# First layer of a decoder trunk: normalize and turn six heads beside the last attention items, and move the last gate section into the norm's gap

## The reference, cut to what matters

```python
mod = silu(c) @ ada_w[i] + ada_b[i]                     # 6 sections of 1024 in a layer
sh_a, sc_a, g_a, sh_f, sc_f, g_f = split(mod, 6)
h = rmsnorm(x, norm_mix[i]) * (1.0 + sc_a) + sh_a
y = diff_attention(h, ...)                              # layer 0
    # 8 heads, 2 blocks of 128 queries each: p = softmax(q k / 8 - slope * dist)
    # o = (p[first] - lam * p[second]) @ v
    # o = rmsnorm(o, subln_g) * (1 - lam_init)          # over the 128 values of one head
    # return o.reshape(B, S, 1024) @ w_out
x = x + g_a * y
h = rmsnorm(x, norm_ffn[i]) * (1.0 + sc_f) + sh_f
x = x + g_f * moe(h, ...)
```

## Time and the profile before

| | |
|---|---|
| time, median of 3 runs | 1453.29 us (1452.13 to 1454.12) |
| time of the profiled execution | 1451.76 us |
| its span | 1450.0 us |
| PE busy | 1328.0 us (92% of the span) |
| DVE, ACT, POOL busy | 550.8, 444.5, 206.1 us |
| read from memory | 514.10 MB |
| mean granted clock of PE | 0.974 of full speed |

### The profile page before, as it was taken

The page is one execution under the profiler, slowest core; times in us unless marked ns, Lnnn a source line. Parts: engine busy times, 40 slices in busy tenths (PEclk is TensorE's granted clock), DMA queues, the critical chain, the costliest instruction groups (busy, mean ns, idle before and its releaser), DMA issues.

```text
span 1450.0 us, 32945 instructions
## 1 busy us (share of the span) xinstructions
PE 1328.0 (92%) x12029; PEld 875.3 (60%) x12030; DVE 550.8 (38%) x1217; ACT 444.5 (31%) x874; POOL 206.1 (14%) x657
## 2 busy tenths in 40 slices
PE   4899678999999999998789999789999999999996
PEld 2788366555455554554489989665555555555553
DVE  2565457233232332222443445473233223322333
ACT  3443333222122222221334454332222222222222
POOL 8000021111111111111000000011111111111110
PEclk9899988999999999999889999999999999999999
DMA  9999992999999999999985534529999999999994
GB/s 345 372 381 399 409 352 81 423 419 423 422 421 422 422 421 422 423 421 421 383 281 181 169 117 146 189 107 422 420 422 421 422 421 422 421 422 422 422 421 204
DMA packets 113082, 516.06 MB, mean 356 GB/s; under 512 B 9368, under 2 KB 46368, under 8 KB 63104
## 3 DMA queue, kind: packets, MB, share of 16 engines
q1 hardware_dynamic: 109920, 509.64, 87.6%
q0 software_dynamic: 2400, 3.49, 0.8%
q10 hardware_dynamic: 704, 2.10, 0.4%
HBM read 514.10 MB, written 1.09 MB: 355 GB/s over the span
## 4 chain that ended last, share of the span: by engine, by line
PE 72%; SPq 8%; DVE 5%; ACT 5%; DMA 5%; issue 3%; POOL 1%; ACTq 1%; DVEq 0%; POOLq 0%
PE bank L882 20%; PE bank L1059 15%; PE bank L1062 7%; PE bank L1080 7%; PE bank L994 6%; PE bank L1035 5%; SPq L336 5%; DMA ring<-in_exp_w_dram 4%; PE bank L1086 3%; PE bank L858 2%; SPq L339 2%; DVE arena L1487 1%; ACT arena L674 1%; DMA ring<-in_da_w_out_dram 1%; PE bank L1069 1%
## 5 line engine op out<-in xcount | busy, mean ns | idle before, releaser
L1059 PE MATMUL bank<-ring,arena 128*64 128x512 f32 x768 | 178.5, 605 | 13.1 <-DMA ring<-in_exp_w_dram 13.1
L1035 PEld LDWEIGHTS bank<-arena 128*128 128x128 bf16 x3264 | 142.1, 98 | 55.5 <-issue 55.0
L994 PE MATMUL bank<-arena_r 128*128 128x512 f32 x560 | 161.1, 418 | 3.0 <-DVE arena_r L1499 3.0
L1499 DVE TENSOR_TENSOR arena_r<-bank,arena_r 128x512 fp32r<-128x512 f32 x136 | 94.1, 692 | 154.1 <-ACT arena_r L686 154.1
L1035 PE MATMUL bank<-arena 128*128 128x64 bf16 (+1 forms) x3264 | 151.8, 207 | 0.0
L679 ACT ACTIVATE arena<-bank 128x256 f32<-128x256 f32 (+1 forms) x68 | 22.6, 333 | 386.9 <-PE bank L1059 269.8
L686 ACT CAST arena_r<-bank 128x512 fp32r<-128x512 f32 x136 | 79.7, 586 | 189.5 <-PE bank L1080 124.8
L994 PEld LDWEIGHTS bank<-arena_r 128*128 128x128 f32 x560 | 94.6, 188 | 60.0 <-issue 47.5
L882 PE MATMUL bank<-HH_r,ring_r 128*128 128x256 f32 x448 | 127.7, 285 | 0.0
L531 POOL TENSOR_TENSOR arena<-arena,pass_base 128x2 f32 x136 | 23.6, 197 | 732.2 <-PE bank L1046 727.1
L1059 PEld LDWEIGHTS bank<-ring,arena 128*64 128x64 f32 x768 | 56.5, 139 | 114.5 <-issue 113.9
(11 more groups left out here) (271 smaller groups left out, 2151.2 us busy)
## 6 DMA issues: line engine op xcount, KB each, us to landing
ring<-in_exp_w_dram SPq DMA_DIRECT2D x264, 1024.0 KB, 24.0
ring<-in_ada_w_dram SPq DMA_DIRECT2D x48, 1024.0 KB, 12.3
HH<-in_exp_w_dram SPq DMA_DIRECT2D x40, 1024.0 KB, 20.4
mods<-in_exp_w_dram SPq DMA_DIRECT2D x40, 1024.0 KB, 24.3
arena<-in_exp_w_dram SPq DMA_DIRECT2D x40, 1024.0 KB, 25.0
ring<-in_ret_w_in_dram SPq DMA_DIRECT2D x24, 1024.0 KB, 11.2
ring<-in_da_w_in_dram SPq DMA_DIRECT2D x12, 1024.0 KB, 16.4
ring<-in_ret_w_out_dram SPq DMA_DIRECT2D x8, 1024.0 KB, 4.9
```

The costliest lines, as they stand in the source:

```text
L994: ins = nc.tensor.matmul(banks[4 + NH * tc + hf][:, :], S[:, P * tc:P * tc + P], y[:, r, 512 * hf:512 * hf + 512], start=False, stop=(last ...
L1035: ins = nc.tensor.matmul(banks[2 - 2 * half][:, P * kk:P * kk + 2 * W], parts[:, tc, r, P * (4 * half + kk):P * (4 * half + kk + 1)], Pg[: ...
L1059: ins = nc.tensor.matmul(banks[1][W * i:W * i + W, :], xg[:, k, W * i:W * i + W], w13[j][:, k, :, :], start=(k == 0), stop=(k == KD - 1))
L1499: nc.vector.tensor_tensor(y[:, 1, 512 * hf:512 * hf + 512], banks[hf][:, :], y[:, 0, 512 * hf:512 * hf + 512], ALU.subtract).then_inc(u[f" ...
```

## The change

Four edits to layer 0, all in the hand-written order.

- **Order of the stream.** `LATER` becomes (0,2), (0,3), (0,4), then the six sections of layer 1, then (0,5), and the four tiles of (0,5) stand behind those of `w_out`. The section itself is computed in `moe` ahead of `turn_h`, once the first half of x is new. Its bias row gets a place of its own (`row5`), DVE adds it behind `low_part("shared", 0, 1)`, and POOL stores and spreads it later.
- **Six heads early.** The mean squares, roots, reciprocals and scaling of heads 0 to 5 (items 0 to 11) are done on ACT and DVE while items 14 and 15 are still under way; PE turns them (`turn_o(0)` to `turn_o(2)`) around `turn_a(15)`. Scaling is now two operations for six heads and two for the last two heads.
- **The projection begins with them.** ACT evicts and rounds the three banks, DVE takes the low parts, and `mix_out` of tile 0 is issued before the last two heads are turned; `turn_o(3)` follows tile 0.
- **Buffers.** The high parts of `w_out` lie in `HH` and `mods` instead of the arena, and bank 0 takes the last two heads.

```diff
-LATER = [(1, s) for s in range(6)] + [(0, 3), (0, 4), (0, 2), (0, 5)]
+LATER = [(0, 2), (0, 3), (0, 4)] + [(1, s) for s in range(6)] + [(0, 5)]
...
-    order += sum(later[6:], [])
-    order += [("mix_out", 0, i) for i in range(4)]
+    order += sum(later[6:9], [])
+    order += [("mix_out", 0, i) for i in range(4)] + later[9]
...
-                ("mix_out", 0): (arena_r[:, 4096:6144], arena_r[:, 10240:12288]),
+                ("mix_out", 0): (HH_r[:, 0:2 * D], mods_r[:, 3 * D:5 * D]),
...
+            ada_bank[9] = banks[4]
+            oT_bank = [banks[i] for i in (1, 2, 3, 0)]
...
-            nc.gpsimd.memset(nrowA, 0.0).then_inc(rows_zero, 1)
+            nc.gpsimd.memset(mods[:, 5 * D:5 * D + 768], 0.0).then_inc(rows_zero, 1)
...
-                               ada_b[0:1].rearrange("a (s q n) -> q a s n", s=6, q=4)[q, :, 2:6]).then_inc(rowsA_in, 16)
+                               ada_b[0:1].rearrange("a (s q n) -> q a s n", s=6, q=4)[q, :, 2:5]).then_inc(rowsA_in, 16)
+                pool.dma_start(row5[32 * q:32 * q + 1, 0, :], ada_b[0:1, 5 * D + 256 * q:5 * D + 256 * (q + 1)]).then_inc(rowsA_in, 16)
...
-            store_rows(1, 0, 6, 6)
-            store_rows(0, 2, 4, 10)
+            store_rows(0, 2, 3, 3)
+            store_rows(1, 0, 6, 9)
             pool.wait_ge(rows_stored, 128)
...
-            pool.wait_ge(o_sumsq, DA_ITEMS)
-            spread(0, 5, gates_in)
...
+            store_rows(0, 5, 1, 10)
+            pool.wait_ge(rows_stored, 192)
+            spread(0, 5, gates_in)
...
+                if l == 0:
+                    release_ada(9)
...
+            load_root_table()
+            act.wait_ge(o_meansq, 1)
+            nc.scalar.activation(early(rs), early(ss), ACT.Sqrt).then_inc(o_root, 1)
             square_o(12)
             release_ada(7)
             evict_aT(14)
             square_o(13)
+            round_w("mix_out", 0, 0)
+            evict_aT(15)
             release_ada(8)
-            evict_aT(15)
-            release_ada(9)
-            load_root_table()
...
+            square_o(14)
             round_w("mix_out", 0, 1)
-            for m in range(4):
+            for m in range(3):
+                evict_oT(m)
+            square_o(15)
+            for m in range(3):
+                round_oT(m)
+            act.wait_ge(o_meansq, 2)
+            nc.scalar.activation(last_heads(rs), last_heads(ss), ACT.Sqrt).then_inc(o_root, 1)
+            mixer_out(0, 0)
+            evict_oT(3)
+            round_oT(3)
+            for i in range(1, 4):
                 mixer_out(0, i)
...
+                if l == 0:
+                    pe.wait_ge(x_new, 1)
+                    ada(*LATER[9], ada_bank[9][:, 0:256])
                 turn_h()
...
-            turn_a(15)
-            later(9)
-            attend(15)
-            pe.wait_ge(o_normed, 1)
-            pe.wait_ge(bank_rows_read, len(LATER))
+            pe.wait_ge(s_ready, DA_ITEMS)
+            pe.wait_ge(o_normed, 1)
+            turn_o(0)
+            turn_a(15)
+            turn_o(1)
+            turn_o(2)
+            attend(15)
+            pe.wait_ge(o_ready, DA_ITEMS)
+            pe.wait_ge(bank_rows_read, 9)
             for i in range(4):
                 mix_out(0, i, 4, da_oT_of)
+                if i == 0:
+                    pe.wait_ge(o_normed, 2)
+                    turn_o(3)
...
+                if l == 0:
+                    later_rows(9)
...
+            mean_squares(early, DA_ITEMS - 4)
             later_rows(6)
             finish_a(14)
             keep_o(13)
             later_rows(7)
             finish_a(15)
+            dve.wait_ge(o_ready, DA_ITEMS - 4)
+            normalize_o(early, slice(0, DA_HEADS - 2), 1)
             keep_o(14)
             later_rows(8)
+            low_part("mix_out", 0, 0)
             keep_o(15)
+            mean_squares(last_heads, DA_ITEMS)
+            for m in range(3):
+                low_oT(m)
             dve.wait_ge(o_ready, DA_ITEMS)
+            normalize_o(last_heads, slice(DA_HEADS - 2, DA_HEADS), 2)
+            low_part("mix_out", 0, 1)
+            low_oT(3)
             low_part("mix_out", 0, 2)
             low_part("mix_out", 0, 3)
```

More of the change, by code:

```diff
@@ L306, in trunk @@
                 turns.append(("ada", 2 * (i // 3) - 2 + i % 3))
-        turns += [("ada", k) for k in range(6, len(LATER))]
+        turns += [("ada", k) for k in range(6, 9)]
         proj0_bank = {i: banks[7 * (n % 2)] for n, (kind, i) in enumerate(turns) if kind == "proj"}
@@ L457, in store_rows @@
                 pool.wait_ge(rows_ready, ready)
-                rows = browA[:, first - 2:first - 2 + count, :] if l == 0 else browB[:, first:first + count, :]
+                rows = browB[:, first:first + count, :] if l == 1 else row5 if first == 5 else browA[:, first - 2:first - 2 + count, :]
                 for q in range(4):
@@ L1522, in later_rows @@
                 if k == 0:
+                    dve.wait_ge(rowsA_in, 16 * 12)
+                if k == 3:
                     dve.wait_ge(rowsB_in, 16 * 12)
[L1524 to L1526 removed]
+                row = browB[:, sec, :] if l == 1 else row5[:, 0, :] if sec == 5 else browA[:, sec - 2, :]
                 dve.wait_ge(ada_done, 2 + k + 1)
```

70 lines of the change are left out of this document (34 added, 36 removed).

## The result

The changed kernel took 1444.22 us (median of 6 runs, 1439.25 to 1448.15) against 1452.79 us of the kernel before (6 runs, 1452.13 to 1454.12). The ratio is 0.9938, 95% interval 0.9918 to 0.9957. Run twice more without any edit, on other chips, it gave 1440.23 and 1443.52, at ratios of 0.9911 and 0.9920. So it is faster by 9 to 13 us, each time with an interval clear of 1. The forecast was 1440.5, within 1437 to 1445.

The account below looks back on a forecast made before the run. It took the weight stream and the serial chain behind `w_out` to bound the kernel ahead of the loop. Terms -12.75 + 0.45 + 0.3 - 1.0 + 0.25 = -12.75 us gave 1440.5 us against the median, range 1437 to 1445.

Parts of the forecast that it names:

- The start of the projection: Output projection of layer 0: starts at 173.6 us, -12.75 us, with the first tile of `w_out` landing at 165.45.
- the tiles follow each other evenly: Rival on the stream into `w_out`: its first tile lands at 164.0, total 1439.0 us; chance 0.15.
- POOL's larger memset: Kernel's opening: last memset grows from 256 to 768 columns, +0.25 us (0 to 0.3); four more small loads hidden.
- The wait before tile 2: Inside the output projection: PE newly waits for tile 2's rounding and low part, +0.3 us, bounds 0 and 1.
- The slow stretch: Projection's first microseconds at clock 0.53 stay as they are; gone entirely saves about 1.9 us, longer costs 0.5.
- `turn_h` at full clock: Transposes after the norm: PE kept busy by the gate section, so they run at full clock, -1.0 us (-1.0 to 0).
- The added row: One addition on DVE of about 0.4 us in the routing's chain: costs 0, up to 0.4 if PE gets ahead.
- PE gets ahead: Rival: logits at full clock gain 0.4 us through the routing, with no slow stretch in the projection; 1438.3 us, chance 0.08.
- The loop keeps its length: Loop over the experts: same length, only starting sooner, so each microsecond saved ahead of it shortens the kernel by one.
- transfers hidden: Rival: `w_out` lands no sooner, only the overlap is gained, -2.5 us; 1450.8 us, chance 0.03.
- the gate section holds everything up: Rival ahead of `turn_h`: late section tiles delay norm, routing and loop; 1457 us or more, chance 0.03 with other waits.
- The gap hurts: Rival in the norm's gap: the section runs at half clock, 7.3 us for 3.66; 1442.8 or 1443.5 us, chance 0.12.

Follow-up runs that it names:

- stream_only: Changed kernel with all eight heads normalized and turned at once behind item 15, as before the change; 1445.10 us, ratio 0.9939.
- heads_only: Changed kernel with the tiles and section (0,5) put back ahead of `w_out`, leaving only the six early heads; 1453.17 us, ratio 1.0000.
- changed_again: Changed kernel without any edit, run beside two repaired kernels on one chip; 1443.52 us, ratio 0.9920.
- pool_start: Changed kernel with POOL's opening block as in the kernel before, the gate row's place zeroed and loaded later; 1443.05 us, ratio 0.9938.
- before_again: Kernel before the change, unedited, run again for a second profiled execution; 1452.44 us, ratio 0.9994.
- later_and_start: Changed kernel with POOL's memset of `y` waiting for `shT` and POOL's opening block as before the change; 1441.30 us, ratio 0.9908.
- after: First profiled execution of the changed kernel, against the kernel before; 1444.57 us, span 1442.8.
- memset_later: Changed kernel with one added line: POOL's memset of `y` waits until DVE has written `shT`; 1442.83 us, ratio 0.9925.
- memset_section: memset_later with the whole gate section waiting for the second half of x instead of the first; 1443.41 us, ratio 0.9926.
- spread_section: later_and_start with the gate section's 64 matmuls in four pieces of 16 over the norm's gap; 1439.85 us, ratio 0.9895.
- before: First profiled execution of the kernel before the change, unedited; 1451.76 us, span 1450.0.
- again: Changed kernel without any edit, once more for a second trace; 1440.23 us, ratio 0.9911, profiled execution 1447.92.
- held: Changed kernel with DVE waiting, ahead of the ranking's two compares, until POOL's iotas are done; 1450.99 us.

## Why the prediction was right, and where its steps failed

**The start of the projection: right, by two errors that cancel, and so by luck.** 173.49 for 173.6, and the first cast at 165.63 for 165.45. ACT's chain is as it was worked out, link by link: second cast 168.19 (168.03), evictions until 171.8 (171.7), 1.49 us from the first rounding to the first matmul. But 165.45 came from leaving the 4.04 us between the two matrices in place. They did not stay. The landings above are 2.5 us apart at that turn in the changed kernel, and in all other kernels with the tiles moved but one (`stream_only`, 3.8). In `heads_only`, with the order of before, the first tile of `w_out` lands 2.4 us behind the last of (0,5), and a step of 3.35 us lies inside (0,5). So the extra 1.5 us belong to no turn between matrices; what they belong to stays open. In the chance of 0.15 for *the tiles follow each other evenly* the mechanism was right. Its time was not: the tile in that place of the stream landed at 163.95 before and at 165.60 after, the stream being 1.65 us behind by then, which the prediction had at nothing. Some of it may go with the later first projection: `changed_again` and `pool_start`, which have that at 40.78 and 40.83, were 0.5 and 1.0 us behind. The rule of the Trainium skill, "DMA: Bandwidth & Descriptors", section "Queues, rings and completion order", by which the prediction had 2.56 us, agrees with the 2.54 us here; the 4.07 of before it does not give.

**POOL's larger memset: term mis-sized, 0.25.** The memset itself grew by 0.43 us (0.45 to 0.88; 0.3 estimated), and the first transposes came 0.35 later, DVE's low parts 0.25. The step that failed is "four more small loads from POOL are hidden". They push POOL's four selects of `decay` from 34.88 to 37.14, beside DVE's low parts of the first weights:

```profile
37.14 4.55 POOL L500 TENSOR_SCALAR_AFFINE_SELECT decay<-decay 128x256 f32<-128x256 f32 x4
```

```profile
35.83 3.21 DVE L1386 TENSOR_TENSOR mods_r<-mods,HH_r 128x512 fp32r<-128x512 f32 x4 [0.57 <-ACT HH_r L618]
38.96 2.48 DVE L1391 TENSOR_TENSOR ring_r<-ring,mods_r 128x2048 fp32r<-128x2048 f32 x1
```

Before, the selects took 2.44 us, the low parts 2.90 and 2.28. Each slows the other, and the first matmul comes 0.25 + 0.31 + 0.20 = 0.76 us later. Over all profiled executions it comes between 40.78 and 42.21 in nine with the larger block (mean 41.41) and between 40.55 and 40.83 in five with the old one (mean 40.74). So the term is 0.7 us on the mean for 0.25, but uneven: `changed_again` has 40.78 with the larger block. With the old block put back (`pool_start`) the selects took 1.91 and the low parts 2.87 and 2.28 again.

**Projection: 24.79 us for 24.4.** The wait before tile 2 is 0.32 (0.3 forecast), the four transposes cost 0.35 (0.45). Of the 1.14 us by which the projection grew, 0.47 are left: tiles 1 and 2 took 5.73 and 5.62 us for 5.44 each, and why stays open. The slow stretch was left as it was, and it was: the 24 matmuls of tile 0 took 7.34 us, the clock back by 177. `before_again` needs 24.72 us without any transposes between, as its clock rose later.

**`turn_h` at full clock: -1.0 not gained in the profiled execution.** It ran in 3.62 us at half clock. The step "PE is now busy until the equivalent of 213.7, so `turn_h` should still find the full clock" holds in some executions only. The 2.33 us of idle time that the prediction itself left behind the section are enough, in six of nine profiled executions, for `turn_h` to run slow. Where the clock holds, it is worth 0.86 us (6.66 from `turn_h` to the logits in `later_and_start`, 7.52 in after), so the size was about right and the certainty wrong.

**The added row, "0, and up to 0.4 if PE gets ahead": the wrong price.** Where PE does not get ahead, the 0.42 us cost nothing: DVE still waits 0.60 us for ACT before `shT` in after (0.81 before). Where PE gets ahead, the 0.42 us are not the price; the collision with POOL's memset is, and that is 3.84 us. The rival *PE gets ahead* (1438.3) therefore had an end that it did not name: a faster PE can make a slower kernel. Two of 17 executions of the changed kernel took 1448; of 19 with the memset behind `shT` (`memset_later`, `memset_section`, `later_and_start`, `spread_section`) none took over 1445.3. None of 19 against two of 17 could also be chance, and that the other long one had the same cause is not shown, as only one was profiled.

**From the logits to the loop, 0.46 us: put at nothing.** PE's first matmuls there ran at half clock until 4.5 us behind their start before, and until 6.1 us in after; PE was through with the up-projections 18.66 us behind the logits' start for 18.21. That is the 0.46.

**"The loop keeps its length": failed, by 1.9 us.** All three executions of the changed kernel need 481.9 to 482.1 from the loop's start to the next projection, both of the kernel before 480.24 and 480.28. In the loop the gathers of 128 columns (L1061) begin some 21 to 31 us apart, 17 times. The first 13 begin within 0.2 us of before's. Then single ones differ, in either direction: the 14th is 1.6 to 1.8 us later in the changed kernel, the 15th 1.3 to 1.4 sooner, the 17th within 0.25 again, and the next projection 1.7 to 1.9 later, while the bytes moved since the loop's start are the same to 0.1 MB at every 40 us. Such steps come between executions of one kernel too: the 16th is at 400.28 in after and at 401.99 in `again`. The moved tiles alone do not explain the end: `spread_section` has them and needs 480.34. What decides these steps stays open.

**Layer 1, 1.9 us, was not in the prediction at all.** Both losses are the clock again. By the one-microsecond stretches, it rises 3.0 and 3.2 us after layer 1's projection begins in the two executions of the kernel before, and 5.5 to 5.7 us after in the three of the changed kernel; at layer 1's logits it rises after 3.4 us in both of before, and after 4.9 to 5.0 in the changed kernel. Over all 14 profiled executions the length goes with the rise: 93.6 to 93.8 us to the retention with a rise after 3.0 to 3.6 us (`before`, `before_again`, `held`, `later_and_start`), 94.6 to 94.7 with one after 5.4 to 5.7 (the ten others). That is shown; what sets the rise is not. `heads_only`, with nothing moved in the stream, has the late one, and `later_and_start`, with everything moved, the early one, so it can be put down to no part of the change that was tried. One to three executions of each kernel are too few to say that it goes with the kernel.

The terms with what was measured: start of the projection -12.86 (forecast -12.75, with +0.25 for POOL apart, which the -12.86 contains), the projection itself +1.14 (+0.75), `turn_h` 0 (-1.0), from the logits to the loop +0.46 (0), behind it +4.06 (0): -7.2 in this pair of executions. Of the 4.5 us in the last two, 2.4 are matmuls at half clock and 1.9 the loop's end. The range reached up to 1445 for other reasons (a gap at half clock, the added row, the wait for tile 2); that the median lies inside it is in part luck. The medians differ by 8.6, 13.3 and 10.9 us on three chips, where the forecast had 12.8: one above, two below. The rivals *transfers hidden* and *the gate section holds everything up* are refuted: `w_out` lands 10.1 us sooner, and PE never waits for the section's tiles. These landed only at 190.3, though, not at 184: between 179.59 and 184.21 another queue, with the small transfers that POOL issues, took 42% of the transfer engines' time, and the tiles came 3.7 to 6.1 us apart. The margin was 8 us, not 14. (That rival's 1457 should read some 1456 by its own terms.) *The gap hurts* did not occur in the change itself (3.66 us, full clock), but was made to occur by a later start (5.35 us).

## What to carry to other kernels

An engine that gets ahead can meet another one that it never met before: for every instruction that becomes free sooner, look at what runs on DVE at that time when POOL is the one released, and tie a long memset to a point behind the short chain that others wait for. Count PE among the engines that can get ahead: its clock may rise 3 or 6 us into the same stretch of matmuls. A short stall on a chain that PE waits for costs more than its own length, since the matmuls behind it may run at half clock; filler work put at one end of the idle time did not keep the clock in most executions here, and four pieces laid over it did in the one that was profiled. Landing times of single transfers settle questions that the waits of an engine hide. And when a gain of 1% is followed through a long kernel, run both kernels a second time with a profile: here half of what was given back late was the moment at which PE's clock rose, which no edit that was tried accounts for.

## What the runs showed of the hardware

- Two VectorE tensor-scalar compares (64 x 64 and 128 x 128) took 2.26 and 2.16 us beside a GpSimd memset of 128 x 2048, and 0.25 and 0.21 without it. With the meeting forced they took 1.69 and 1.59, and ended 0.05 and 0.12 us behind the memset. A TENSOR_SCALAR of 1 x 32 and a cast of 128 x 128 took 0.57 and 0.70 beside it, 0.17 and 0.36 without; TENSOR_TENSOR and TENSOR_REDUCE kept their times.
- A select of 128 x 256 on GpSimd took 0.41 us alone, 0.84 to 0.94 beside VectorE's subtractions of 128 x 512, and 2.44 beside one of 128 x 2048. The subtractions took 0.88 in place of 0.68, and 2.48 in place of 2.28.
- The same 2.33 us of idle TensorE, at the same place, were followed by 16 transposes in 3.62 us in one execution and 2.19 in another; after 2.64 us idle 64 matmuls took 5.35 in place of 3.66; across gaps of 1.57 and 0.45 the clock stayed at 2.4 GHz.
- After idle time the granted clock rose 2.8 to 6.2 us into a stretch of dense matmuls, and not at the same place in two executions of one kernel: 3.0 and 6.1 us into the logits of the changed kernel. A rise 2.7 us later was worth 1.2 us in layer 1's projection (94.74 for 93.56).
- The last tile of one matrix and the first of the next, 1 MB each in one queue that never ran dry, landed 4.07 us apart in one kernel and 2.54 in another; other neighbours landed 2.56 apart.
- In the loop, with equal bytes moved to 0.1 MB, single gathers began 1.3 to 1.9 us sooner or later in one execution than in another, of the same kernel too, and the next ones in step again.
